# Token sides of 256 and 264 columns in place of two of 260, and their matmuls given the columns in sweeps

## What is computed

```python
h = rmsnorm(x, norm_mix_g);  proj = h @ w_in            # 2048 -> 3072
...                                                     # RG-LRU heads and pooling heads, per head
x = x + y_mix @ w_out                                   # 2048 -> 2048
h2 = rmsnorm(x, norm_mlp_g); f = relu(h2 @ w_up)        # 2048 -> 8192
x = x + (f * f) @ w_down                                # 8192 -> 2048
y = rmsnorm(x, norm_final_g)
```

## Time and profile before

| | |
|---|---|
| median of 3 runs | 1841.91 us (1840.62 to 1842.90) |
| span of the profiled execution | 1841.4 us; the profile gives no other time for it |
| PE busy | 1812.1 us, 98% of the span, 15,016 matmuls |
| DVE busy | 1478.1 us, 80% |
| ACT busy | 924.6 us, 50% |
| HBM | 222.00 MB read, 64.53 MB written |

### The profile page before, as it was taken

How to read it: one execution, slowest core, us unless ns; L and a number is a source line. 1 busy time by engine, 2 the same in 40 slices (tenths; PEclk the granted TensorE clock), 3 DMA queues, 4 the chain that set the end, 5 groups by cost and what they waited for, 6 DMA issues and landing times. The chain is left out here.

```text
span 1841.4 us, 38079 instructions
## 1 busy us (share of the span) xinstructions
PE 1812.1 (98%) x15016; PEld 1805.0 (98%) x15016; DVE 1478.1 (80%) x2039; ACT 924.6 (50%) x1322; POOL 132.9 (7%) x224
## 2 busy tenths in 40 slices
PE   7999999999999999999999999899999999999998
PEld 7999999999999999999999999899999999999998
DVE  7777785545488888888888888899888888889897
ACT  6555533333344454454445445555555555556565
POOL 3000000200000000000000000110000000001100
PEclk9999999999999999999999999999999999999999
DMA  8333333344354444544444452788666776767742
GB/s 275 103 92 91 97 98 93 116 152 139 99 171 148 160 146 163 173 135 156 148 161 146 143 173 90 213 233 238 185 179 179 199 181 181 192 168 206 230 114 93
DMA packets 209979, 288.19 MB, mean 157 GB/s; under 512 B 9437, under 2 KB 186089, under 8 KB 209808
## 3 DMA queue, kind: packets, MB, share of 16 engines
q1 hardware_dynamic: 185552, 186.75, 33.0%
q0 software_dynamic: 23984, 99.19, 18.7%
q10 hardware_dynamic: 288, 0.11, 0.0%
HBM read 222.00 MB, written 64.53 MB: 156 GB/s over the span
## 5 line engine op out<-in xcount | busy, mean ns | idle before, releaser
L897 PE MATMUL ps<-forms,u_high 128*128 128x260 f32 x2688 | 490.4, 282 | 0.7 <-DVE product_parts L1833 0.7
L897 PEld LDWEIGHTS ps<-forms,u_high 128*128 128x128 f32 x2688 | 413.0, 188 | 0.9 <-issue 0.9
L897 PE MATMUL ps<-forms,u_low 128*128 128x260 f32 x1344 | 374.8, 282 | 0.6 <-DVE u_low L1823 0.6
L897 PE MATMUL ps<-forms,d_high 128*128 128x260 f32 x2240 | 373.6, 283 | 1.0 <-DVE product_parts L1833 1.0
L897 PEld LDWEIGHTS ps<-forms,d_high 128*128 128x128 f32 x2240 | 314.4, 188 | 1.2 <-ACT d_high L1180 1.1
L897 PE MATMUL ps<-f_forms,d_high 128*128 128x260 f32 x1344 | 265.4, 283 | 4.2 <-ACT d_high L1180 1.6
L897 PEld LDWEIGHTS ps<-forms,u_low 128*128 128x128 f32 x1344 | 250.7, 188 | 0.8 <-DVE u_low L1823 0.8
L1363 DVE TENSOR_TENSOR w_low<-raw,w_high 128x512 fp32r<-128x512 f32 x160 | 109.0, 689 | 137.0 <-ACT w_high L992 135.8
L897 PEld LDWEIGHTS ps<-f_forms,d_high 128*128 128x128 f32 x1344 | 204.9, 188 | 6.7 <-ACT d_high L1180 3.7
L897 PE MATMUL ps<-forms,d_low 128*128 128x260 f32 x1120 | 192.5, 283 | 0.0
L992 ACT ACTIVATE w_high<-raw 128x512 fp32r<-128x512 f32 x160 | 99.4, 628 | 180.7 <-PE ps L704 174.6
(11 more groups left out here) (305 smaller groups left out, 3578.5 us busy)
## 6 DMA issues: line engine op xcount, KB each, us to landing
even_rows<-in_w_up_dram SPq DMA_DIRECT2D x32, 1024.0 KB, 5.6
odd_rows<-in_w_up_dram SPq DMA_DIRECT2D x32, 1024.0 KB, 5.8
d_even<-in_w_down_dram SPq DMA_DIRECT2D x33, 768.0 KB, 7.1
d_odd<-in_w_down_dram SPq DMA_DIRECT2D x33, 768.0 KB, 5.2
raw<-in_w_in_dram SPq DMA_DIRECT2D x96, 256.0 KB, 2.7
sums_spill<-part_out POOLq DMA_DIRECT2D x40, 520.0 KB, 5.4
scratch<-f_spill POOLq DMA_DIRECT2D x20, 910.0 KB, 7.1
f_spill<-f_out POOLq DMA_DIRECT2D x32, 520.0 KB, 4.7
```

What stands on the lines that cost most here:

```text
L897: mm = pe.matmul(out, w[:, k, :], x[:, form, :], start=(PRODUCT_OPENS[r] and at == 0), stop=at == len(steps) - 1, skip_group_check=True)
```

## The change

The two token sides become 264 columns each (SIDE): 256 prompt tokens and, as a tail, the 8 samples. Both sides carry the samples in the stage's input, but only four of the seven products use the tail: the forms of A11, S1, S3 and A22 are multiplied with 264 columns, those of A12, S4 and S2 with 256 (PRODUCT_COLS). For the tail the four products are plain block products, so the sums are set up accordingly: two small copies in `x2_sums` and two in `f_sums` put sample columns where the scheme would have put differences, and the tail of the bank that holds S2's product is cleared once per buffer (`clear_tail`), for which PE waits on a new semaphore twice. In the output projection the sides are 256 and 264. The input projection keeps 260 and 260.

Every matmul of the output projection and of the up and down projection gets its columns, and its output in PSUM, in another order (`by_lines`): runs of 4 columns (16 bytes), and from run to run a step of 4 runs (256 columns, four sweeps over the side) or of 3 runs (264 columns, three sweeps). The number of matmuls stays. The filler has 28 matmuls of 256 columns in place of 14 of 512. Buffers grow to fit; `rstd`, `scratch` and `ones` change their shape.

```diff
+SIDE = HALF_COLS + SAMPLES
+WIDE = 2 * SIDE
-WARM = 14 * (512,) + 24 * (128,)
+WARM = 28 * (256,) + 24 * (128,)
+PRODUCT_COLS = (SIDE, SIDE, HALF_COLS, SIDE, HALF_COLS, HALF_COLS, SIDE)
+SWEEPS = {HALF_COLS: 4, SIDE: 3}
...
-            def unit(n, j, buf, high, low):
+            def by_lines(columns):
+                sweeps = SWEEPS.get(columns.shape[-1])
+                return columns.rearrange("p (m n e) -> p n m e", n=sweeps, e=4) if sweeps else columns
+
+            def unit(n, j, buf, high, low, cuts=(0, HALF, TOK)):
...
-                            out = ps[:, 4 * buf + 2 * t + a, 0:HALF]
-                            pe.matmul(out, wh, high[:, k, a * HALF:(a + 1) * HALF], start=first, stop=False)
+                            out, at = ps[:, 4 * buf + 2 * t + a, 0:cuts[a + 1] - cuts[a]], slice(cuts[a], cuts[a + 1])
+                            pe.matmul(by_lines(out), wh, by_lines(high[:, k, at]), start=first, stop=False)
...
             def out_unit(o, j, buf):
-                unit(IN_PAIRS + o, j, buf, y_high, y_low)
+                unit(IN_PAIRS + o, j, buf, y_high, y_low, (0, HALF_COLS, TOK))
...
-                out = ps[:, bank_at, 0:HALF]
+                out = by_lines(ps[:, bank_at, 0:PRODUCT_COLS[r]])
...
+                if m == 1 and r == 5:
+                    pe.wait_ge(tails_clear, 2)
...
-                    mm = pe.matmul(out, w[:, k, :], x[:, form, :], start=...
+                    mm = pe.matmul(out, w[:, k, :], by_lines(x[:, form, 0:PRODUCT_COLS[r]]), start=...
...
             pe.wait_ge(s_hi, 2)
+            pe.wait_ge(tails_clear, 1)
             for n in WARM:
-                x = s_high[0][:, S3:S3 + (2 if n > HALF else 1), 0:min(n, PROMPT // 2)]
+                x = s_high[0][:, S3, 0:n]
...
-                dve.tensor_tensor(v, ps[:, 4 * (o % 2):4 * (o % 2) + 4, 0:HALF].rearrange(...), v,
-                                  ALU.add).then_inc(pair_evac, 1)
+                sides = ps[:, 4 * (o % 2):4 * (o % 2) + 4, :].rearrange("p (k a) t -> p k a t", a=2)
+                dve.tensor_tensor(v[:, :, 0, 0:HALF_COLS], sides[:, :, 0, 0:HALF_COLS], v[:, :, 0, 0:HALF_COLS], ALU.add)
+                dve.tensor_tensor(v[:, :, 1, :], sides[:, :, 1, 0:SIDE], v[:, :, 1, :], ALU.add).then_inc(pair_evac, 1)
...
                 step(dve.tensor_tensor(s2, s1, a11, ALU.subtract))
-                step(dve.tensor_tensor(a21, a11, a21, ALU.subtract))
+                step(dve.tensor_tensor(a21[:, 0:HALF_COLS], a11[:, 0:HALF_COLS], a21[:, 0:HALF_COLS], ALU.subtract))
+                step(dve.tensor_copy(a21[:, HALF_COLS:SIDE], a22[:, HALF_COLS:SIDE]))
                 settle()
+                step(dve.tensor_copy(a11[:, HALF_COLS:SIDE], s1[:, HALF_COLS:SIDE]))
...
+            def clear_tail(o):
+                dve.wait_ge(pair_evac, o + 5)
+                dve.memset(ps[:, 4 * (o % 2) + BANK_D, HALF_COLS:SIDE], 0.0).then_inc(tails_clear, 1)
```

More of the change, by code:

```diff
@@ L140 @@
 HALF_COLUMNS = ((0, 2), (2, 5))
-H_HIGH_AT, H_LOW_AT, WORK_AT, Y_HIGH_AT, Y_LOW_AT = (n * KC * TOK * 4 for n in range(5))
-W_AT = 5 * KC * TOK * 4
+ARRAY, FORM_SET, PAIR_BYTES = KC * TOK * 4, FORMS * SIDE * 4, 2 * WIDE * 4
+STAGE_AT = 6 * 2 * FORM_SET
+H_HIGH_AT, H_LOW_AT, WORK_AT = (n * ARRAY for n in range(3))
+Y_HIGH_AT = STAGE_AT + 2 * PAIR_BYTES + 4 * SIDE * 4
+Y_LOW_AT = Y_HIGH_AT + ARRAY
+W_AT = Y_LOW_AT + ARRAY + 64
 AUX_AT = W_AT + 3 * RING * UNIT * 4
@@ L237, in build @@
         pool_last = at_byte("pool_last", LAST_AT + (4 + 2 * SAMPLES) * HEADS * 4, [P, POOL_BUF + SAMPLES, HEADS])
[L241 to L246, removed]
+        x2 = [at_byte(f"x2_{b}", STAGE_AT + b * PAIR_BYTES, [P, 2, WIDE]) for b in range(2)]
+        blocks = at_byte("blocks", STAGE_AT + 2 * PAIR_BYTES, [P, 4, SIDE])
+        sums = at_byte("sums", AUX_AT + 2 * UNIT * 4, [P, 3, SIDE])
+        sets = [at_byte(f"forms{o}", o * 2 * FORM_SET, [P, 2, FORMS, SIDE], F32R) for o in range(6)]
+        late_high, late_low = (at_byte(f"forms67_{part}", at, [P, 2, FORMS, SIDE], F32R)
                                for part, at in (("high", Y_HIGH_AT), ("low", Y_LOW_AT)))
@@ L425, in slot_of, with token_tile @@
             return d_high[q % SLOTS][:, 0:end - first, :], d_low[q % SLOTS][:, 0:end - first, :]
+        def token_tile(t):
+            return slice(t // 2 * SIDE + t % 2 * P, t // 2 * SIDE + t % 2 * P + P)
         def halves(v):
@@ L696, in unit @@
                         for a in range(2):
-                            out = ps[:, 4 * buf + 2 * t + a, 0:HALF]
-                            pe.matmul(out, wh, high[:, k, a * HALF:(a + 1) * HALF], start=first, stop=False)
+                            out, at = ps[:, 4 * buf + 2 * t + a, 0:cuts[a + 1] - cuts[a]], slice(cuts[a], cuts[a + 1])
+                            pe.matmul(by_lines(out), wh, by_lines(high[:, k, at]), start=first, stop=False)
                         for a in range(2):
-                            out = ps[:, 4 * buf + 2 * t + a, 0:HALF]
-                            pe.matmul(out, wh, low[:, k, a * HALF:(a + 1) * HALF], start=False, stop=False)
+                            out, at = ps[:, 4 * buf + 2 * t + a, 0:cuts[a + 1] - cuts[a]], slice(cuts[a], cuts[a + 1])
+                            pe.matmul(by_lines(out), wh, by_lines(low[:, k, at]), start=False, stop=False)
                         for a in range(2):
-                            out = ps[:, 4 * buf + 2 * t + a, 0:HALF]
-                            mm = pe.matmul(out, wl, high[:, k, a * HALF:(a + 1) * HALF], start=False, stop=last)
+                            out, at = ps[:, 4 * buf + 2 * t + a, 0:cuts[a + 1] - cuts[a]], slice(cuts[a], cuts[a + 1])
+                            mm = pe.matmul(by_lines(out), wl, by_lines(high[:, k, at]), start=False, stop=last)
                 mm.then_inc(unit_used, 1)
@@ L896, in product @@
                     w, x = wl if kind == 2 else wh, tiles[k][1 if kind == 1 else 0]
-                    mm = pe.matmul(out, w[:, k, :], x[:, form, :], start=(PRODUCT_OPENS[r] and at == 0), stop=at == len(steps) - 1,
+                    mm = pe.matmul(out, w[:, k, :], by_lines(x[:, form, 0:PRODUCT_COLS[r]]), start=(PRODUCT_OPENS[r] and at == 0), stop=at == len(steps) - 1,
                                    skip_group_check=True)
@@ L915, in _ @@
                             for t in range(2):
-                                mm = pe.matmul(ps[:, 4 + a, 0:HALF], ones[:], scratch[:, 2 + t, a * HALF:(a + 1) * HALF],
+                                mm = pe.matmul(ps[:, 4 + a, 0:SIDE], all_ones, wide[:, 2 + t, a * SIDE:(a + 1) * SIDE],
                                                start=(t == 0), stop=(t == 1))
@@ L930, in totals @@
                     for a in range(2):
-                        mm = pe.matmul(ps[:, 0, col + t:col + t + 1], scratch[:, tiles + a, t * P:(t + 1) * P], ones[:, 0:1],
+                        mm = pe.matmul(ps[:, 0, col + t:col + t + 1], wide[:, tiles + a, token_tile(t)], ones[:, 0:1],
                                        start=(a == 0), stop=(a == 1))
@@ L1882, in _ @@
             squares_add(OUT_PAIRS - 1)
+            clear_tail(OUT_PAIRS - 1)
             def f_scale(m):
```

139 lines of the change are left out of this document (72 added, 67 removed).

## The result

The changed kernel takes **1818.52 us** (median of four runs, 1818.04 to 1820.81) where the kernel before took 1841.68 (1840.62 to 1842.90 with one more run of it): 23.2 us less, a ratio of 0.9874 [0.9857, 0.9890] (the brackets hold the 95% interval, here and below). It is faster, as forecast, and inside the outer range of 1,743 to 1,847; but it lies outside the forecast's own range of 1,745 to 1,790, in that of the first rival. The forecast was 75 us, and less than a third of it came.

A forecast was written before the change was run, and what follows sets the result against it. PE bounds the kernel: matmul count times start-to-start distance, 120.1 ns per 260 columns. Gain 79.9 - 4 - 0.5, less about 0.5 in waits, is 75 us: 1,767 us, own range 1,745 to 1,790 (57%), outer 1,743 to 1,847.

The forecast's parts named there:

- the first rival: Whole kernel: DVE late or many collisions stay, so half the gain, 1,804 us (1,790 to 1,838); 16%.
- the price of a swept matmul: Up, down and output projections: 113.5 and 113.4 ns per swept matmul, saving 71.0 and 8.9 us, 79.9 us in all.
- the collisions: PE's column and weight streams getting in each other's way in SBUF, read as the 8.8 ns lost per 260-column matmul.
- The ones matmuls: Plain float32 matmuls of 260 columns at half rate: 219.7 ns each, only 3.0 ns over two clocks per column.
- the loss and its floor: Per 260-column matmul: 3.0 ns fixed, 8.8 lost streaming; best case 112 ns for 256 columns, 113.0 for 264.
- Columns: Up and down projection: 0.57 columns more per matmul, 0.25 ns each, costing 2.7 us on 10,752 matmuls.
- Give-back: Near the end, where DVE is busiest, half of an 8.2 us gain counted as lost: 4 us back.
- DVE and ACT: Up projection: DVE 93% busy, covered by its 87.0 us of waits for ACT, which would halve.
- The turn of the stages: Between output and up projection: some 0.5 us more before the first low weights; filler change nothing; `tails_clear` waits hidden.
- Nothing happens to the rate: Swept matmuls: loss is a limit on lines per time, order doesn't matter; 1,845 us, +0.17%; 13%.
- Sweeps cost: Swept matmuls: each jump between runs costs one clock, 27 ns more per matmul, 332 us more, 2,175 us; 14%.
- Half of it comes: The first rival's title: DVE late or a good part of the collisions stays; 1,804 us, 1,790 to 1,838; 16%.

The follow-up runs named there:

- e5: e1 with each up and down projection weight load reading one weight column 128 times: 1836.71 us, 117.4 ns (256 columns) and 120.5 ns (264).
- e16: The changed kernel, sweeps kept, with each up and down projection weight load reading one weight column 128 times: 1802.28 us, 113.9 and 117.7 ns.
- e9: e1 with every up and down projection matmul streaming one column 256 or 264 times, weight loads unchanged: 1776.26 us, 112.2 and 113.3 ns.
- e3: The changed kernel with sweeps kept for columns read from SBUF but PSUM written in order: 1820.07 us, 115.6 and 119.8 ns.
- e4: The changed kernel with columns read from SBUF contiguously and only PSUM written in sweeps: 1847.92 us, 118.6 and 122.0 ns.
- e1: The changed kernel without sweeps, its 256 and 264 columns read and written contiguously: 1848.12 us, 118.7 and 122.0 ns.
- e2: The changed kernel with eight sweeps for 256 columns (128-byte steps) and six for 264 (96-byte steps): 2161.52 us, 124 and 164 ns.

## Why the prediction was part right and part wrong

- **The step that failed is the price of a swept matmul**: "I take 113.5 and 113.4, close to the best." It measures 119.7 for 264 columns and 115.6 for 256, 117.9 as the mean of the seven products (4 x 119.7 + 3 x 115.6, over 7), and 117.0 in the output projection. With these the forecast's own sum is 2.2 x 10,752 + 2.2 x 1,536 = 27 us in place of 79.9. The reason given for taking the best end, "once the collisions are gone little is left", named the wrong partner: the weight stream's share is 1.3 to 2.0 ns (e5, e16), and sweeps leave it as it is. The rest is the column stream's own walk from line to line, which sweeps change but don't remove: 3.4 and 6.4 ns are left over e9 with the weights' share in it. The ones matmuls did show that neither writing nor issue costs more than 3 ns, and e9 bears that out; they could not show what walking in sweeps costs at full rate. The text had said "No row shows a matmul in sweeps" and "The rows don't prove it"; the point was put near one end of an open range all the same, where the middle of rival one lay closer.
- **Right: the loss and its floor.** 8.8 ns lost as columns stream, 3.0 ns fixed: with one column the loss is gone, 112.2 and 113.3 ns (e9) for the forecast 112 and 113.0. e9's 1776 us, less the 8.9 that the forecast had for the output projection (not swept in e9), is the forecast's 1,767, but by luck: its products are faster than forecast, 112.8 ns on the mean for 113.5, some 8 us, and PE waits 12 us longer than in e1 for the 4 set aside. The Trainium skill's "TensorE: Matmul & The Clock Gate", section "Back-to-back issue gap", has N / 2.4 + 2.5 ns for an isolated matmul, 109.2 and 112.5 here: e9 comes within 0.8 ns of it with 264 columns (113.3), the swept kernel doesn't (119.7). **Right: where.** The reading of SBUF alone makes the gain (e3, e4). The input projection stayed at 421 matmuls in 50 us.
- **Columns**: 2.7 us forecast, 5.8 measured for all stages (e1). In e1 the mean of the seven products is 120.6 ns against 120.2 before, 0.4 ns where the slope gave 0.25; what else of the 5.8 us is columns wasn't taken apart. Small beside the rest.
- **Give-back.** 4 us were set aside for the end of the down projection against a gain of 75. Already a gain of some 27 loses about 3: the down projection gained 4.7 us less than the up projection, and some 1.7 of that is the clock (below). The gaps over 260 ns grew by 1.6 us in its first 110 us and by 1.7 from 1650 us on, so only half of it lies where the forecast looked. The waits of PE from 500 us on and the end of the chain in the changed kernel:

```profile
PE ps L917 <- DVE product_parts L1865: 5.4, 8, 1.3
PE ps L917 <- ACT product_parts L1234: 2.2, 1, 2.2
PE ps L917 <- DVE d_low L1855: 2.2, 3, 1.6
...
PE ps L917 <- DVE u_low L1855: 0.8, 1, 0.8
```

```profile
1764.99 0.44 DVE product_parts L1865
...
1765.56 23.64 PE ps L917 x198
```

  Against the earlier trace rows the wait for `product_parts` has doubled from 2.6 us. The last run of PE begins behind DVE in both kernels, here at 1765.56 with 198 matmuls in place of 372; it goes on with 54 more after no time lost. So half of rival one's mechanism (DVE late) is there, with a few us. Had the rate come as forecast, more would have gone: e9 lost 24.6 - 12.3 = 12.3 us in waits more than e1, three times the 4 of the sum.
- **DVE and ACT.** DVE's waits from 550 to 1150 us were to halve from 87.0:

```profile
DVE u_low L1855 <- ACT u_high L1201: 67.2, 117, 1.3
```

  They fell by 20 us of the 43, with a third of the gain in rate. The cover held in the up projection.
- **The turn of the stages.** From the filler to the first product 510.62 to 516.49 before, 505.75 to 511.65 now: 5.87 and 5.90 us, nothing, as forecast for the filler. PE's wait for the first low weights, on which some 0.5 us were to fall, went from 0.64 to 0.8 us. No wait of PE on `tails_clear` shows.
- **The rivals.** "Nothing happens to the rate" is out by ten matmuls in 50 us. "Sweeps cost" didn't happen here, but it lay one step size away: with six and eight sweeps it is 2161.5 us, close to the 2,175 that its text gave (e2), though by certain steps, in SBUF or in PSUM, and not by a price per jump. "Half of it comes" has the measured time in its range (1,804, from 1,790 to 1,838), and its second cause, that "a good part of the collisions stays", is the nearer one, though what stays is mostly no collision with the weights. Of the signs that the text set, the input projection kept its count; the clock did fall below 1.00 in one slice, which cost 1.7 us (at the end).

What stays open: why three lines in turn run free and four don't, why 96 bytes is the worst step measured, and whether that step costs in SBUF or in PSUM. Lines that lie in parts of SBUF that can't be read in quick succession would do that; no run here lays such parts out, so it is only an idea, and one for the losses in SBUF alone.

## What to carry to other kernels

When a stream of fp32r matmuls runs some 10% over a column per clock, stream one and the same column first: a single run splits the loss into what the walk over SBUF costs and what an order could win back at most. Then measure each step size by itself, because 64 bytes gained 3 ns of 256 columns and 96 bytes cost some 40 of 264, and keep runs of four columns, since runs of two took nearly twice the time. Change the order on one side alone, SBUF or PSUM, if you want to know which of them costs. And with an engine behind at 85 to 95% of the time, look at what the next bound gives back before counting the rate in full: here both ends of the down projection.

## What the runs showed of the hardware that was not expected

- The order of columns in PSUM was free in runs of four with steps of 64 and 48 bytes (e4: 118.6 and 122.0 ns, as contiguous), while the same order in SBUF alone took 256 columns from 118.7 to 115.6 ns (e1, e3), at the same number of lines read.
- A matmul over 16 columns again and again (122.2 ns, 256 columns) is slower than one over 12 (113.7 ns, 264 columns).
- In one slice of 10 us the granted clock dropped, which the digits of the earlier trace rows don't show, since a 9 stands for 90% or more; so "full" in every slice said more than they do. It dropped in the profiled execution of before at 40 us, and of after at the start of the down projection. Before, then after:

```profile
40.00:50.00 10.00, 8.52 (x56) 8.21 (x56) 7.14 (x18) 6.02 (x9) 2.13 (x4) 0.83 0.88 275
```

```profile
1150.00:1160.00 10.00, 6.91 (x49) 5.75 (x47) 7.89 (x18) 5.26 (x13) 0.00 (x0) 1.00 0.57 185
1160.00:1170.00 10.00, 9.71 (x68) 9.63 (x69) 8.55 (x20) 7.01 (x15) 2.34 (x3) 0.83 0.88 231
```

  0.83 means 3.4 of 10 us at the lower level, 1.2 GHz; PE had been busy for 6.91 of the 10 us ahead in the changed kernel. At half the rate for 3.4 us that is 1.7 us. It took that much off the gain of the down projection, and the input projection, without it, ended 1.5 us sooner than before: together nothing in these two executions, and so no part of the 23.2 us.
